# Two-layer decode step on one core: output weights fetched ahead, ScalarE and VectorE steps in another order, and TensorE's half key unit inside the prompt step

## The chip, the core and the metric

The kernel runs on one core of one Trainium2 chip. The metric is the device time of one execution in microseconds (us). Before the change it is 2687.8 us, the median of 3 runs (2681.95 to 2691.65).

## The reference, cut to what matters

Two layers; each computes a token branch (pooling in layer 0, stick-breaking attention in layer 1), a cross-attention over 256 memory tokens, gates both and projects the result back to the model width. The prompt has 1024 tokens; the sample group has 8 sequences of 4 tokens, each with 2048 past tokens whose keys and values lie in a paged cache.

```python
def sb_block(q_blk, qpos_blk, k, v, kpos, bias):
    z = einsum('bqhd,bkhd->bhqk', q_blk, k) * (HEAD_DIM ** -0.5) + bias
    mask = kpos[None, :] < qpos_blk[:, None]
    log_beta = log_sigmoid(z)
    log_rem = where(mask, log_beta - z, 0.0)
    later = cumsum(log_rem, axis=3, reverse=True) - log_rem
    a = where(mask, exp(log_beta + later), 0.0)
    return einsum('bhqk,bkhd->bqhd', a, v)

def merge_out(branch, gate, mq, mgate, mk, mv, g_q, w_out):
    q = rms_norm(mq, g_q)
    p = softmax(einsum('bqhd,bmhd->bhqm', q, mk) * (HEAD_DIM ** -0.5))
    mo = einsum('bhqm,bmhd->bqhd', p, mv)
    y = concatenate([branch * silu(gate), mo * silu(mgate)], axis=-1)
    return y @ w_out          # (tokens, 2048) @ (2048, 1024)
# x = x + merge_out(...), in both layers, for prompt and samples
```

There are 12 heads of width 128 in layer 1. Everything is float32; products that need it are made as three products of a rounded high part and a low rest (`hi*hi`, `lo*hi`, `hi*lo`).

## The kernel before, in words

The program runs phase after phase. Layer 0: input projection and pooling, `memory_attention_phase`, `out_phase`. Layer 1: `norm_phase`, `in_phase` (the projection, keys and values), `memory_attention_phase`, `stick_phase`, `out_phase`. Each phase is a block in which the five engines run their own program and wait on semaphores; the next block begins when all have ended. SyncE (SP) issues nearly all DMAs, in program order, so that a wait in its queue holds back everything behind it.

**out_phase** (L1182) is y @ w_out + x for 9 tiles of 128 tokens. TensorE multiplies 16 slices (`kk`) of the contraction, for each two halves of 512 columns with three products: 96 matmuls a tile. First `load_y(0)` fetches tile 0 of y and x; then w_out comes in 8 pieces of 1 MB through two buffers (`w`); ScalarE writes the high part of each piece (`w_hi`, L1241) and VectorE the rest (`w_lo`, L1254); the same is done for y once a tile (L1237, L1249). The weights are kept for all tiles. TensorE waits for `ylo` and, in tile 0, for each piece's `wlo`. A tile is loaded into the one buffer `y` when the rest of the tile before has been taken. Nothing of this begins before the phase.

**memory_attention_phase** (L794) fetches memory keys and values of the samples and, behind them, calls `following.fetch(sp)`: in layer 0 `NothingAhead`, in layer 1 `StickAhead` (L1476), which fetches what stick_phase needs first: the page table, query and key rows of head 0, the first key units (`keys`), then `vh`, `gh` and the new tokens' `kn`, `qn`, `vn`, the other key units and value pages. Its tile loop on ScalarE has exponentials (L975) of tile t+2, the copy of sample values `vev` (L991), and in every second tile the copy of the turned probabilities `pT` (L931); VectorE takes the other `pT` copies (L1051), the row maxima (L1017), the division (L1032) and the gate (L1038).

**stick_phase** (L1548) lays prompt and sample work side by side by one list `order`, written out before the program. The prompt has 144 steps P0 to P143, 12 for each head, of 128, 256, 384, 512, 128, 256, 384 columns and then five times 512. A step is: scores z of step t+2 (L2012), the triangle products which sum log terms (L2039, L2041 for the block before, L2046, L2049 for this one), and values of step t-1 (L2028). ScalarE does `evacuate(t+2)` (L1761, L1763: two reads of the score bank), `log_part(t+1)` (L1769, L1771), `high(t+1)` (L1789, rounded part of `spl`) and the exponential of step t (L1782). VectorE does `softplus(t+1)` (L1852), `exponent(t)` (L1870) and `low(t+1)` (L1861). For the samples there are 64 key units K in two halves (24 matmul pairs each, L2065, keys times queries into the one bank `krow`), the copy of that bank by ScalarE (`rows_out`, L1795, semaphore `rev`), its turning T (L2085), and 128 value pages V (6 matmuls each, L2107). One key unit goes with two prompt steps, so K lasts over P0 to P127; V begins at P14. SP fetches keys when VectorE has turned a unit (`ktr`) and a value page when TensorE has used one (`vdone`). The first half of K(u+1) overwrites `krow` and so waits for `rev` of unit u:

```python
                        if u:
                            pe.wait_ge(s["rev"], u)
```

The new tokens' scores (`new_tokens`, L2125) stand behind the first key half unit.

## Time and profile before

| | us |
|---|---|
| median of 3 runs | 2687.8 (2681.95 to 2691.65) |
| the profiled execution | 2685.2 |
| its span, first instruction to last | 2683.4 |
| memory attention of layer 0, TensorE's tiles | 609 to 673 |
| out_phase, layer 0: SP's first DMA, TensorE's first matmul, tile 1, end | 682.1, 696.2, 730.1, 905 |
| memory attention of layer 1, to its end | 1742 |
| stick_phase, TensorE | 1750.1 to 2447.5 |
| out_phase, layer 1: SP's first DMA, TensorE's first matmul, end | 2456.1, 2470.1, 2683 |
| TensorE busy | 2418.1 (90%) |
| VectorE, ScalarE busy | 988.4 (37%), 861.4 (32%) |

Times in the rows further down are counted from the start of the span. In a timeline row the first number is the start, the second how long the instruction (or the group under x) took, and in brackets stands the engine's idle time before it with what ended it. A matmul's duration includes its way through the array, so starts tell the pace better than durations. TensorE has 864 matmuls in each out_phase.

### The profile page before, as it was taken

How to read it: one execution, taken by the hardware profiler on the slowest of the kernel's cores; microseconds unless marked ns; L12 is line 12 of the kernel's file. 1: busy time of each engine (PE TensorE's matmuls, PEld its weight loads, DVE VectorE, ACT ScalarE, POOL GpSimd, SP SyncE). 2: the span in 40 equal slices, each digit the busy share in tenths (PEclk: the TensorE clock that was granted, in tenths of full speed). 3: DMA queues.
4: the chain of work that ended last, by engine and by line, in shares of the span. 5: the costliest groups of instructions: out<-in, count | busy, mean ns of one | idle time of the engine just before them, and what ended most of it. 6: DMA issues, size and time to landing. Idle time of an engine off the chain costs nothing. (4 is left out here: it accounts for less than half of the span.)

```text
span 2683.4 us, 42572 instructions
## 1 busy us (share of the span) xinstructions
PE 2418.1 (90%) x17253; PEld 2002.8 (75%) x17253; DVE 988.4 (37%) x1469; ACT 861.4 (32%) x1662; POOL 185.6 (7%) x377
## 2 busy tenths in 40 slices
PE   4699999998599699999999999779999999995999
PEld 4699999896488589999999998655555555542787
DVE  5421334105311321111112111467777777753211
ACT  4321111114210222112110011356666666674100
POOL 0000000102000000000001120211211111110000
PEclk8899999999799789999999998879999999998999
DMA  5422201302633232233231122658999999973432
GB/s 173 136 81 82 82 18 34 112 2 102 231 99 95 100 113 81 98 128 130 94 121 58 45 88 79 191 173 319 362 370 385 369 384 365 364 252 132 141 96 71
DMA packets 203708, 426.34 MB, mean 159 GB/s; under 512 B 22965, under 2 KB 116257, under 8 KB 203497
## 3 DMA queue, kind: packets, MB, share of 16 engines
q1 hardware_dynamic: 193209, 387.58, 41.3%
q0 software_dynamic: 10304, 36.05, 3.6%
q8 instruction: 136, 2.23, 0.3%
q14 instruction: 59, 0.48, 0.1%
HBM read 361.75 MB, written 62.37 MB: 158 GB/s over the span
## 5 line engine op out<-in xcount | busy, mean ns | idle before, releaser
L80 PE MATMUL o_bank<-o_w_hi,o_y_hi 128*128 128x512 f32 x576 | 228.9, 397 | 60.4 <-DVE o_w_lo L1254 59.5
L81 PE MATMUL o_bank<-o_w_lo,o_y_hi 128*128 128x512 f32 x576 | 227.4, 395 | 0.0
L82 PE MATMUL o_bank<-o_w_hi,o_y_lo 128*128 128x512 f32 x576 | 227.0, 394 | 0.0
L80 PEld LDWEIGHTS o_bank<-o_w_hi,o_y_hi 128*128 128x128 f32 x576 | 110.0, 191 | 88.8 <-issue 46.7
L1902 DVE STREAM_TRANSPOSE b_kt<-bf_kraw 128x768 f32<-128x768 f32 x172 | 166.2, 967 | 0.0
L1378 ACT ACTIVATE i_stage<-i_bank 128x352 f32<-128x352 f32 x108 | 50.1, 465 | 347.9 <-PE i_bank L82 347.9
L2065 PEld LDWEIGHTS b_krow<-b_kt,b_qd 128*32 128x32 f32 x3072 | 105.3, 111 | 70.0 <-issue 54.8
L80 PE MATMUL i_bank<-h_hT_hi,h_w_hi 128*128 128x352 f32 x432 | 140.7, 326 | 2.1 <-PEq L75 2.1
L2012 PE MATMUL b_zbank<-bf_qh,bf_kh 128*128 128x512 f32 (+3 forms) x288 | 134.2, 549 | 8.5 <-PEq L75 8.5
L80 PE MATMUL i_bank<-h_hT_hi,i_w_hi 128*128 128x352 f32 x432 | 141.1, 327 | 0.0
L2065 PE MATMUL b_krow<-b_kt,b_qd 128*32 128x128 f32 x3072 | 140.9, 280 | 0.0
L82 PE MATMUL i_bank<-h_hT_hi,i_w_lo 128*128 128x352 f32 x432 | 140.1, 324 | 0.0
L82 PE MATMUL i_bank<-h_hT_hi,h_w_lo 128*128 128x352 f32 x432 | 139.5, 323 | 0.0
L81 PE MATMUL i_bank<-h_hT_lo,h_w_hi 128*128 128x352 f32 x432 | 139.3, 323 | 0.0
L81 PE MATMUL i_bank<-h_hT_lo,i_w_hi 128*128 128x352 f32 x432 | 139.3, 322 | 0.0
L2107 PE MATMUL b_vout<-bf_vpage,b_daw 128*32 128x512 f32 x768 | 132.6, 597 | 0.0
L1237 ACT ACTIVATE o_y_hi<-o_y 128x2048 fp32r<-128x2048 f32 x18 | 34.5, 1916 | 297.4 <-DMA o_y<-scratch_yT 297.4
L1852 DVE SCALAR_TENSOR_TENSOR b_spl<-b_z,b_soft 128x512 f32<-128x512 f32 (+2 forms) x144 | 80.4, 558 | 127.9 <-ACT b_soft L1771 66.9
L82 PEld LDWEIGHTS o_bank<-o_w_hi,o_y_lo 128*128 128x128 f32 x576 | 110.1, 191 | 23.2
L2012 PEld LDWEIGHTS b_zbank<-bf_qh,bf_kh 128*128 128x128 f32 x288 | 44.3, 193 | 111.0 <-issue 108.7
L81 PEld LDWEIGHTS o_bank<-o_w_lo,o_y_hi 128*128 128x128 f32 x576 | 110.0, 191 | 22.8
L2028 PE MATMUL b_obank<-b_a,bf_vh 128*128 128x512 f32 (+3 forms) x288 | 119.3, 496 | 0.6 <-ACT b_a L1782 0.6
(308 smaller groups left out, 5567.0 us busy)
## 6 DMA issues: line engine op xcount, KB each, us to landing
bf_vpage<-in_cache_sb_v_dram SPq DMA_DIRECT2D x128, 768.0 KB, 7.2
bf_kraw<-in_cache_sb_k_dram SPq DMA_DIRECT2D x172, 384.0 KB
l_w<-in_cache_sb_k_dram SPq DMA_DIRECT2D x84, 384.0 KB
o_y<-scratch_yT SPq DMA_DIRECT2D x18, 1024.0 KB, 6.6
o_w<-in_w_out_dram SPq DMA_DIRECT2D x16, 1024.0 KB
l_w<-in_w_in_sb_dram SPq DMA_DIRECT2D x8, 1536.0 KB
i_w<-in_w_in_sb_dram SPq DMA_DIRECT2D x8, 1536.0 KB
l_w<-in_cache_mem_k_dram SPq DMA_DIRECT2D x16, 512.0 KB, 4.3
```

The source lines that it names most:

```text
L80: pe.matmul(out, stat_hi, mov_hi, start=first, stop=False)
L81: pe.matmul(out, stat_hi, mov_lo, start=False, stop=False)
L82: return pe.matmul(out, stat_lo, mov_hi, start=False, stop=last)
L1237: act.activation(y_hi[t % 2][:, :, :], y[:, :, :], ACT.Copy).then_inc(s["yhi"], 1)
L1378: act.activation(stage[:, b % 2, unit(n)], bank[(b % 2) * 3 + n][:, 0:TT], ACT.Silu if kind == "gate" else ACT.Copy).then_inc(s["evac"], 1)
L1852: dve.scalar_tensor_tensor(out=spl[:, 0:n], in0=z[:, t % 3, 0:n], scalar=0.0, in1=soft[:, t % 2, 0:n], op0=ALU.max, op1=ALU.add).then_inc( ...
L1902: dve.transpose(kt[u % 2][:, :, :, x * Q:(x + 1) * Q].rearrange("p h f j -> p (h f) j"), kraw[u % NK][:, x, :].rearrange("p (f j) -> p f j ...
L2012: ins = pe.matmul(zbank[t % 2][:, 0:n], kh[:, h % 2, kb * P:(kb + 1) * P], qh[:, h % 2, q0:q0 + n], start=True, stop=not diag, skip_group_ ...
L2028: pe.matmul(obank[:, 512 - n:512], vh[:, h % 2, kb, :], a[:, t % 3, 0:n], start=first, stop=last, skip_group_check=True).then_inc(s["pvd"], 1)
L2065: ins = pe.matmul(krow[pair * CT:(pair + 1) * CT, 0:P], qd[:, i % 2, at:at + CT], kt[u % 2][:, h, f, :], start=odd == 0 and f == 0, stop=o ...
L2107: ins = pe.matmul(vout[m * CT:(m + 1) * CT, :], daw[:, at, m * CT:(m + 1) * CT], vpage[n % NV][:, m * VC:(m + 1) * VC], start=n % PAGES == ...
```

## The change

- `out_phase` takes w_out in 16 pieces of 512 KB through five buffers (`RAW`): three lie in the layer's input weight buffer, which is free by then, two in a shared `Arena`. In `OutAhead.fetch` five pieces and 12 of the 16 slices of y's tile 0 (eight DMAs, 3.25 MB) are fetched ahead, and two pieces (`SPLIT`) and those slices are split ahead (`high` on ScalarE, `low` on VectorE). In layer 0 this stands in the memory attention: the fetch behind the memory DMAs, the splitting at the end of tiles t = 2 to 6. In layer 1 the fetch stands in stick_phase's SP list behind P130, ScalarE's part at P133 to P137, VectorE's at P134 to P138. The last four slices (in layer 1 slices 10 and 11, of the last head's two halves) come in out_phase.
- In `out_phase` the load of y's and x's tile 1 stands between pieces 10 and 11, its splitting before piece 13, and x's tile 0 last.
- `StickAhead.fetch` no longer fetches `vh`, `gh`, `kn`, `qn`, `vn`; `fetch_rest` does it as SP's first work in stick_phase.
- The buffers `kraw` and `kt` of stick_phase lie in the `Arena`.
- ScalarE's step is now log_part(t+1), exponential of t, high(t+1), evacuate(t+2); VectorE's takes exponent(t) before softplus(t+1).
- TensorE takes scores(t+2) alone, then the half key unit, then the rest of the step.

```diff
@@ class OutAhead
+        self.order = list(range(KM)) if i == 0 else list(range(10)) + [12, 13, 14, 15, 10, 11]
+        self.early, self.late = [([(0, 4), (4, 8), (8, 12)], (12, 16)), ([(0, 5), (5, 10), (12, 16)], (10, 12))][i]
+    def fetch(self, sp):
+        for at in range(SPLIT):
+            self.weights(sp, at)
+        for r in self.early:
+            self.rows(sp, r, self.yl)
+        for at in range(SPLIT, RAW):
+            self.weights(sp, at)
+    def high(self, act, t):
+        n = t - 2
+        if 0 <= n < SPLIT:
+            act.wait_ge(self.wl[n], 16)
+            act.activation(self.w_hi[n][:, :], self.w[n], ACT.Copy).then_inc(self.whi, 1)
+        if SPLIT <= n < SPLIT + len(self.early):
+            act.wait_ge(self.yl, 16 * len(self.early))
+            a, b = self.early[n - SPLIT]
+            act.activation(self.y_hi[:, a:b, :], self.y[:, a:b, :], ACT.Copy).then_inc(self.yhi, 1)
+    def low(self, dve, t):
+        n = t - 2
+        if 0 <= n < SPLIT:
+            dve.wait_ge(self.whi, n + 1)
...
@@ out_phase, SP
-                load_y(0)
-                for j in range(NW):
-                    if j >= 2:
-                        sp.wait_ge(s["wlo"], j - 1)
-                    sp.dma_start(w[j % 2][:, :, :], A["w_out"][i, j * CH * P:(j + 1) * CH * P, :].rearrange(
-                        "(k p) n -> p k n", p=P)).then_inc(wl[j % 2], 16)
-                load_y(1)
+                begun.rows(sp, begun.late, s["yl"])
+                for at in range(RAW, KM):
+                    sp.wait_ge(begun.wlo, at - RAW + 1)
+                    begun.weights(sp, at)
+                    if at == 2 * RAW:
+                        load_y(1)
+                load_x(0)
@@ out_phase, ScalarE (VectorE alike)
-                part(0)
-                for j in range(NW):
+                for at in range(SPLIT, KM):
+                    if at == RAW:
+                        part(0)
+                    if at == KM - 3:
+                        part(1)
@@ memory_attention_phase, end of a tile
+                    following.high(act, t)
+                    following.low(dve, t)
@@ stick_phase, SP
+                begun.fetch_rest(sp)
                 sp.dma_start(gs[:, :, :], S["gT"][:, :, SEQ:T].rearrange("h p t -> p h t")).then_inc(s["gsl"], 16)
+                    if e == ("P", NSTEP - 14):
+                        sp.wait_ge(s["ktr"], PG * NU)
+                        for n in range(2):
+                            sp.wait_ge(ys[n], 16 * 5)
+                        out.fetch(sp)
@@ stick_phase, ScalarE
                 def step(t):
-                    if t + 2 < NSTEP:
-                        evacuate(t + 2)
                     if t + 1 < NSTEP:
                         log_part(t + 1)
-                    if t + 1 < NSTEP:
-                        high(t + 1)
                     n = steps[t][4]
                     act.wait_ge(s["tsub"], t + 1)
                     act.activation(a[:, t % 3, 0:n], a[:, t % 3, 0:n], ACT.Exp).then_inc(s["ax"], 1)
+                    if t + 1 < NSTEP:
+                        high(t + 1)
+                    if t + 2 < NSTEP:
+                        evacuate(t + 2)
@@ stick_phase, VectorE
+                    exponent(t)
                     if t + 1 < NSTEP:
                         softplus(t + 1)
-                    exponent(t)
@@ stick_phase, TensorE
-                for e in order:
+                for n, e in enumerate(order):
                     if e[0] == "P":
-                        step(e[1])
+                        if e[1] + 2 < NSTEP:
+                            scores(e[1] + 2)
+                        if order[n + 1:n + 2] == [] or order[n + 1][0] != "K":
+                            step(e[1])
                     if e[0] == "K":
                         unit(e[1], e[2])
+                        if order[n - 1][0] == "P":
+                            step(order[n - 1][1])
```

TensorE in stick_phase, one step of 512 columns with a half key unit and a value page; before (`b_zbank` is the score bank, `b_cbank` the triangles' sum, `b_obank` the values, `b_krow` the key unit, `b_vout` the value page):

```order
L2012 MATMUL b_zbank<-bf_qh,bf_kh 128x512
L2039 MATMUL b_cbank<-b_spl_hi,b_before_r 128x512
L2041 MATMUL b_cbank<-b_spl_lo,b_before_r 128x512
L2046 MATMUL b_cbank<-b_spl_hi,b_suffix_r 128x512
L2049 MATMUL b_cbank<-b_spl_lo,b_suffix_r 128x512
L2028 MATMUL b_obank<-b_a,bf_vh 128x512
L2065 MATMUL b_krow<-b_kt,b_qd 32x128 x12
L2107 MATMUL b_vout<-bf_vpage,b_daw 32x512 x3
```

The same stretch now (the keys read from the arena):

```order
L2125 MATMUL b_zbank<-bf_qh,bf_kh 128x512
L2176 MATMUL b_krow<-ar_arena,b_qd 32x128 x12
L2150 MATMUL b_cbank<-b_spl_hi,b_before_r 128x512
L2152 MATMUL b_cbank<-b_spl_lo,b_before_r 128x512
L2157 MATMUL b_cbank<-b_spl_hi,b_suffix_r 128x512
L2160 MATMUL b_cbank<-b_spl_lo,b_suffix_r 128x512
L2141 MATMUL b_obank<-b_a,b_vh 128x512
L2218 MATMUL b_vout<-bf_vpage,b_daw 32x512 x3
```

The half key unit went from behind the values to between the scores and the triangles.

ScalarE in stick_phase, from a step's logarithm to the copy of a key unit (`b_soft`, `b_z` the two reads of the scores, `b_spl_hi` the rounded part, `b_a` the exponential, `b_kev` the key unit's copy); before:

```order
L1771 ACTIVATE b_soft<-b_soft 128x512
L1789 ACTIVATE b_spl_hi<-b_spl 128x512
L1782 ACTIVATE b_a<-b_a 128x512
L1795 ACTIVATE b_kev<-b_krow 96x128
L1799 ACTIVATE b_dx<-b_dx 128x384
```

Now:

```order
L1878 ACTIVATE b_soft<-b_soft 128x512
L1885 ACTIVATE b_a<-b_a 128x512
L1896 ACTIVATE b_spl_hi<-b_spl 128x512
L1868 ACTIVATE b_soft<-b_zbank,c_rowb 128x512
L1870 ACTIVATE b_z<-b_zbank,c_rowb 128x512
L1902 ACTIVATE b_kev<-b_krow 96x128
L1906 ACTIVATE b_dx<-b_dx 128x384
```

The rounded part and the two reads of the next scores now stand between the exponential and the copy of the key unit.

ScalarE in layer 0's memory attention, now (`a_e` the exponentials of a tile's four heads, `a_pT` a copy of turned probabilities, `a_vev` a copy of sample values, `ar_w_hi` and `ar_y_hi` high parts of a weight piece and of slices of y):

```order
L975 ACTIVATE a_e,a_sums<-a_bank,a_nb,a_st 128x256 x4
L1243 ACTIVATE ar_w_hi_4487<-l_w 128x1024
L931 ACTIVATE a_pT<-a_bank 128x512
L975 ACTIVATE a_e,a_sums<-a_bank,a_nb,a_st 128x256 x4
L991 ACTIVATE a_vev<-a_bank 128x512
L1243 ACTIVATE ar_w_hi_4488<-l_w 128x1024
L931 ACTIVATE a_pT<-a_bank 128x512
L975 ACTIVATE a_e,a_sums<-a_bank,a_nb,a_st 128x256 x4
L1247 ACTIVATE ar_y_hi<-ar_arena 128x512
```

Before, the same rows stand there without L1243 and L1247.

## Rows read from the trace of the kernel before

**Rows 1.** The page: busy time by engine; the 40 slices of the span.

```profile
PE 2418.1 (90%) x17253; PEld 2002.8 (75%) x17253; DVE 988.4 (37%) x1469; ACT 861.4 (32%) x1662; POOL 185.6 (7%) x377
...
GB/s 173 136 81 82 82 18 34 112 2 102 231 99 95 100 113 81 98 128 130 94 121 58 45 88 79 191 173 319 362 370 385 369 384 365 364 252 132 141 96 71
```

**Rows 2.** Busy time by stretch; behind POOL: granted PE clock, DMA share, GB/s.

```profile
2048.00:2335.00 287.00, 274.54 (x3277) 155.90 (x3265) 212.21 (x339) 191.31 (x417) 42.50 (x109) 1.00 0.98 375
...
2102.86:2160.30 57.44, 54.86 (x667) 31.48 (x664) 43.17 (x70) 38.23 (x84) 5.60 (x13) 1.00 0.97 362
```

**Rows 3.** What SP's queue waited for, 1850 to 2350: us in total, times, longest.

```profile
SPq L1511 <- PE b_vout L2107: 139.4, 56, 4.2
```

**Rows 4.** Timeline, out_phase of layer 0: SP, ScalarE, TensorE.

```profile
682.11 0.38 SPq L1209 DMA_DIRECT2D o_y<-scratch_yT  x1
...
694.39 1.91 ACT L1241 ACTIVATE o_w_hi<-o_w 128x2048 fp32r<-128x2048 f32 x1 [0.62 <-DMA o_w<-in_w_out_dram]
...
696.24 0.76 PE L80 MATMUL o_bank<-o_w_hi,o_y_hi 128*128 128x512 f32 x1 [23.22 <-DVE o_w_lo L1254]
...
727.62 0.39 PE L81 MATMUL o_bank<-o_w_lo,o_y_hi 128*128 128x512 f32 x1
...
729.21 0.39 PE L82 MATMUL o_bank<-o_w_hi,o_y_lo 128*128 128x512 f32 x1
730.06 0.50 PE L80 MATMUL o_bank<-o_w_hi,o_y_hi 128*128 128x512 f32 x1 [0.46 <-DVE o_y_lo L1249]
```

**Rows 5.** Timeline, out_phase of layer 1: SP, TensorE, VectorE.

```profile
2456.05 0.38 SPq L1209 DMA_DIRECT2D o_y<-scratch_yT  x1
...
2470.10 0.77 PE L80 MATMUL o_bank<-o_w_hi,o_y_hi 128*128 128x512 f32 x1 [22.62 <-DVE o_w_lo L1254]
...
2502.99 2.29 DVE L1249 TENSOR_TENSOR o_y_lo<-o_y,o_y_hi 128x2048 fp32r<-128x2048 f32 x1 [1.28 <-ACT o_y_hi L1237]
```

**Rows 6.** Timeline of VectorE, memory attention of layer 0.

```profile
652.17 0.69 DVE L1051 COPY a_pT<-a_bank 128x512 f32<-128x512 f32 x1 [0.18 <-PE a_bank L1165]
```

**Rows 7.** Timeline, memory attention of layer 1: TensorE, SP.

```profile
1720.50 3.64 PE L1131 MATMUL a_bank<-a_sq,a_psT 128*32 128x512 f32 x16 [8.05 <-DMA a_sq<-in_cache_mem_v_dram]
...
1686.43 0.44 SPq L1526 DMA_DIRECT2D bf_vh<-out_sbv_p_dram  x1
...
1695.01 4.09 SPq L1506 DMA_DIRECT2D bf_kraw<-in_cache_sb_k_dram  x4
...
1706.84 3.19 SPq L948 DMA_DIRECT2D a_sq<-in_cache_mem_v_dram  x4
```

**Rows 8.** Timeline of TensorE, stick_phase.

```profile
1758.52 1.49 PE L2125 MATMUL b_sbank<-bf_vpage 128*32 128x32 f32 x24
...
2150.61 1.13 PE L2012 MATMUL b_zbank<-bf_qh,bf_kh 128*128 128x512 f32 x2
...
2152.50 1.02 PE L2028 MATMUL b_obank<-b_a,bf_vh 128*128 128x512 f32 x2
2153.45 0.97 PE L2065 MATMUL b_krow<-b_kt,b_qd 128*32 128x128 f32 x21
...
2158.44 1.07 PE L2065 MATMUL b_krow<-b_kt,b_qd 128*32 128x128 f32 x24
2159.34 1.03 PE L2107 MATMUL b_vout<-bf_vpage,b_daw 128*32 128x512 f32 x6
2160.30 0.49 PE L2012 MATMUL b_zbank<-bf_qh,bf_kh 128*128 128x128 f32 x2
```

**Rows 9.** Timeline, stick_phase: ScalarE (first row the key copy), then VectorE.

```profile
2161.15 0.25 ACT L1795 ACTIVATE b_kev<-b_krow 96x128 f32<-96x128 f32 x1
...
2434.91 0.63 ACT L1789 ACTIVATE b_spl_hi<-b_spl 128x512 fp32r<-128x512 f32 x1 [0.81 <-DVE b_spl L1852]
...
2439.29 0.63 ACT L1789 ACTIVATE b_spl_hi<-b_spl 128x512 fp32r<-128x512 f32 x1 [0.81 <-DVE b_spl L1852]
...
2439.17 0.68 DVE L1870 TENSOR_TENSOR b_a<-b_z,b_cbank 128x512 f32<-128x512 f32 x1
```

More of the change, by code:

```diff
@@ L1194, in out_phase @@
         x = k.sb("x", [P, 2, D])
         bank = k.ps("bank", 4)
-        wl = [k.sem(f"wl{n}") for n in range(2)]
         xl = [k.sem(f"xl{n}") for n in range(2)]
         ol = [k.sem(f"ol{n}") for n in range(2)]
-        s = {n: k.sem(n) for n in "yl whi wlo yhi ylo ready added".split()}
+        s = {n: k.sem(n) for n in "yl yhi ylo ready added".split()}
         N = TILES + 1
-        NW = KM // CH
         tok = lambda t: t * P if t < TILES else LAST
+        part_of = lambda t: slice(0, KM) if t else slice(*begun.late)
@@ L1614, in stick_phase @@
         a = k.sb("a", [P, 3, 512])
-        kt = [k.sb(f"kt{n}", [P, HH, HD // Q, P]) for n in range(2)]
         qd = k.sb("qd", [P, 2, HEADS * QP])
```

168 lines of the change are left out of this document (117 added, 51 removed).

## The prediction

> **What bounds the kernel now.** I read the page first: TensorE is busy 90% of the span [rows 1], so time can be won only where it stands still or where its own work shrinks, and the change removes no matmul. Then the stretches: in the long middle of stick_phase TensorE is busy 274.5 of 287 us, ScalarE two thirds, VectorE three quarters, and the DMA engines show a share of 0.98 at 375 GB/s [rows 2]. So there both TensorE and the transfers are near full. The queue's waits say which leads: SP waits 139 us of 500 for TensorE to have used a value page before it may fetch the next [rows 3]; the transfers wait for the compute, not the reverse. Then the timelines at the seams: TensorE stands 23.2 us ahead of out_phase in layer 0 [rows 4] and 22.6 us in layer 1 [rows 5], both for the first rest of a weight piece, and 8.05 us in layer 1's memory attention for a DMA [rows 7]. These are the large holes. A difference of 0.3%, 8 us, is about what a measurement of this kernel can tell from none.
>
> **The change part by part**, in us against the profiled execution (2685.2; the median is 2.6 above it).
>
> *Memory attention, layer 0: +6.* New there: two weight pieces and 12 slices of y, each split in ScalarE and VectorE. ScalarE takes 1.91 for 1 MB [rows 4], so about 0.95 for a piece and 0.48 to 0.5 for four slices of y; VectorE's rest takes 2.29 for 1 MB [rows 5], so 1.15 and 0.6. VectorE's rest of tile t waits for ScalarE's high part, which stands behind that engine's exponentials of tile t+2; behind VectorE's rest stands its copy of the turned probabilities, which today starts 0.18 after it has nothing else to do [rows 6], and TensorE waits for that copy. Walking the five tiles gives 1.3, 3.3, 0, 2.3 and 0.4 behind t = 2 to 6; sum 7.3, less about 1 which the tiles that ScalarE copies give back: 6. Bounds: 0 if the slack in the tiles takes all, and 9, all five high parts and rests in a row (2 times 2.1 and 3 times 1.1 is 7.5) and the DMA issues behind them.
>
> *out_phase, layer 0: -18.* SP begins at 682.11, TensorE at 696.24, and tile 1 starts at 730.06 [rows 4]. Now two pieces and y are ready, and TensorE begins at about 682.3. The pace is 7 matmuls in 1.59, 0.227 each [rows 4], 21.8 for 96. But it needs data: still to come are 11 pieces of 0.52 MB, 0.26 MB of y, and 1.57 MB for tile 1, 7.6 MB. The 3.67 MB before were issued at 682.11 and the last was there at 694.39 [rows 4]: 299 GB/s with the start-up in it, and 385 GB/s is the highest slice of the page [rows 1]. That is 20 to 25 us, and the split of the last piece (0.95 and 1.15) and its six matmuls (1.4) come after it: 705.6 to 711 for the end of tile 0. Five buffers pass slowly where piece 11 waits behind tile 1's y and x (1.57 MB, 4.5 us) and where tile 1's split (1.91 and 2.29) stands before piece 13; walked through buffer by buffer it gives 5.6 of stalls above 21.8 and a slow start of 1.8 to 2: 711.7. So 730.06 becomes about 712, -18. Bounds -24 (no stall) and -8 (start at the full 14 us earlier, half of it lost to the supply).
>
> *Memory attention, layer 1: -6.* SP issued vh, gh, kn, qn, vn from 1686.43 to 1695.01, about 8 with their waits, and only at 1706.84 the next memory values [rows 7], for which TensorE waited until 1720.50, idle 8.05 [rows 7]. They go out 8 earlier, so the idle shrinks to about 2; the rows behind are unchanged. Bounds -8 and 0.
>
> *Start of stick_phase: +2.* The moved loads are now the block's first DMAs, and new_tokens at 1758.52 [rows 8] needs three of them. Issued from 1750 on, five DMAs in some 8 us as before, they land near 1760.5. Bounds 0 and +6.
>
> *P0 to P13: 0*, between -3 and +3: no value pages, TensorE waits for the first steps' chain anyway, and this chain has the same members.
>
> *P14 to P127, keys and values: +13.* This is the term that decides least clearly. The new order of ScalarE puts the rounded part of step t+1 and two reads of step t+2 between the exponential and the key copy; the new order of TensorE puts the next key half unit ahead of the triangles. The first half of K(u+1) waits for the copy of K(u). So a loop arises over a pair of steps. From K(u+1)'s first half: 0.90 (2158.44 to 2159.34) [rows 8], triangles 0.93, values 0.95 (2152.50 to 2153.45), turned rows 0.3, a value page 0.96 (2159.34 to 2160.30), scores and triangles of the next step 1.89 (2150.61 to 2152.50) and the second half unit 0.90: 6.84. From there to the copy: semaphore 0.20, exponent to exponential 0.72 (from 2439.17 to the end of the rounded part that starts at 2439.29, 0.6), the exponential 0.6, rounded part 0.6 and two reads of 0.6 less what they overlap, 1.14 (between 2434.91 and 2439.29 there are six such instructions and 0.81 idle, 0.6 each) [rows 9], the copy 0.25 [rows 9] and semaphores 0.17: 3.6. The loop is 10.4 for two full steps; TensorE took 9.69 for them from 2150.61 to 2160.30 [rows 8]. With the narrower steps of a head the same walk gives 8.9, 8.6, 8.9, 9.7, 10.4 and 9.4, 55.9, and with the sample sums (2.25) and the select (0.7), which stand in the loop too, 58.8 against 57.44 [rows 2]: +1.4 a head, 9.5 heads, +13. Bounds: below, the idle of a head (57.44 less 54.86 [rows 2], 2.6) vanishes, which is what the new order of the exponent and of ScalarE gives if the copy never comes late, -25; above +25, if every head loses a further 1.3 to bubbles. I take the walk, since it rests on durations of these same instructions.
>
> *P128 to P143: -3.5.* Without keys ScalarE sets the pace: 4.38 a full step, of which 0.81 is a wait for spl [rows 9]. With the exponential of t before the rounded part the wait is covered: 3.77, 0.6 a step, -8 over ten full and six narrower. Against it ScalarE gets two pieces (0.95 each) and three parts of y (0.65, 0.65, 0.55): 3.75, and VectorE a little: +4.5. The 3.25 MB fetched at P130 take about 9 us of transfers ahead of the last pages; SP has some five steps of pages in buffers (19 to 22 us), so it stays hidden. If it did not, +4.
>
> *out_phase, layer 1: -19.5.* As in layer 0, from 2456.05; tile 0 took until 2505.3 (the rest of y at 2502.99 and its 2.29) [rows 5]. 2456.2 and 29.5 is 2485.7. Bounds -25 and -9.
>
> *Blocks and semaphore clears: +1.* A few more clears of some 0.1 each.
>
> Sum: 6 - 18 - 6 + 2 + 0 + 13 - 3.5 - 19.5 + 1 = -25. Against the median: 2662.8, rounded to **2662**.
>
> **A rule against the trace.** In the middle of stick_phase the trace shows 375 GB/s over 287 us and slices up to 385 [rows 1, 2]. The Trainium skill, "DMA: Bandwidth & Descriptors", section "Where 436 GB/s comes from", says that for transfers between HBM and SBUF the HBM side binds, at about 358 GB/s for a core. The trace does not agree: it lies 5% over it. By that rule the stretch could gain nothing from any order of instructions, which is the second rival below, reached by another way.
>
> **The rivals.**
> - *The copy never comes late.* The six steps' buffers and the half unit's 0.9 cover the copy, and TensorE runs without gaps. For: the walk has 0.7 of lateness in the full pairs and little in the narrow ones. Against: TensorE's busy 95% leaves 2.6 a head, and at this pace pages would have to come at 375 times 57.4/54.9, 392 GB/s, above every slice of the page. Price -25 for +13: total -63, **2625**.
> - *The stretch does not move.* Transfers at a share of 0.98 [rows 2] set the pace whatever TensorE does, or lateness and gain cancel. For: share and rate; against: SP's 139 us of waits for TensorE [rows 3]. Price 0 for +13: **2650**.
> - *Supply limits both out starts.* The pieces of 512 KB come no faster than those of 1 MB, and tile 0 is as long as before, only begun 14 earlier. Then each start gains 14 less some loss, 13: about 11.5 less gain in the two: **2674**.
> - *Slower: the half key unit lengthens each step's own loop.* Triangles of step t+1 now always have 0.90 of key work before them, and the loop triangle, exponent, exponential, rounded part, rest runs through every step. Where the loop already bounds, 0.4 of the 0.9 (the rest covers what TensorE waited for) comes on each of 114 steps, +46 for +13: total +8, **2695**. It decides once the rounded part's chain, 3.5 to 3.6, together with the key half and triangles exceeds the step of 4.8 that TensorE needs itself [rows 8]; 3.6 and 1.8 is 5.4, but only if the chain begins behind the triangles and not, as I read the order, from the step before. Against it: log and reads of a step are two steps ahead.
> - That the change does not do what it says (the early pieces not ready at the out start) would leave the starts as they are: part of the third.
>
> **How the numbers follow.** My forecast 0.52; no move of the stretch 0.20; TensorE without gaps 0.10; supply 0.10; the slower case 0.08. The forecast alone spans 2648 to 2676 (its terms' bounds taken two at a time). The range should hold 8 in 10: it takes in the stretch unmoved and the supply case and leaves out the two ends: 2638 to 2682. Faster by over 0.3% is below 2679.7: the forecast, the second, the first and most of the supply case: 0.86. Within 0.3%: 0.08, from the upper tails of the forecast and of supply. Slower: 0.06, most of the last case.
>
> **What would show it.** TensorE's first matmul of either out_phase within 1 us of SP's first DMA there, and tile 1 some 29 us later. In the middle of stick_phase a new idle of TensorE ahead of the first key half, released by ScalarE's copy, about 0.7 in full pairs, and heads of 58.8 with SP waiting more for TensorE than now; heads of 54.9 would prove the first rival, heads of 57.4 the second, and idle ahead of the triangles (for the rest of spl) in every step the slower case. In the tail full steps of 3.8. In memory attention of layer 0 five idles of TensorE behind VectorE's or ScalarE's split, together 6; in layer 1 an idle of 2 for 8. I am wrong if the middle moves by more than 25 either way, or if an out start gains less than 8.

## The result: slower by 0.7%, with the half key unit as the cause

| | before | after |
|---|---|---|
| median of 5 runs, us | 2687.8 (2681.3 to 2691.7) | 2705.0 (2696.9 to 2711.2) |
| ratio | | 1.0068, 95% interval 1.0042 to 1.0095 |
| profiled execution, us | 2685.2 | 2711.2 |
| its span, us | 2683.4 | 2709.5 |

The prediction was 2662 in a range of 2638 to 2682, with 0.06 for slower: it was wrong in sign and size. The profiled execution after lies 6 us above its median, the one before 2.6 below; the comparison of the two traces (26.1 us of span) therefore overstates the change by some 9 us.

Two rows of the page after, the answer to [rows 1]. TensorE is busy 38 us longer with the same 17253 matmuls, and the slices of the middle moved 331 to 365 GB/s where they had moved 362 to 385.

```profile
PE 2455.7 (91%) x17253; PEld 2006.6 (74%) x17253; DVE 988.4 (36%) x1491; ACT 857.7 (32%) x1684; POOL 188.9 (7%) x377
...
GB/s 171 136 79 81 81 26 25 111 22 130 184 93 101 103 111 95 111 104 127 95 115 58 66 55 153 216 173 301 343 337 365 331 364 334 349 247 193 144 100 65
```

The waits of TensorE after, from 1850 to 2350 (us in total, times, longest):

```profile
PE b_krow L2176 <- ACT b_kev L1902: 35.6, 29, 2.3
```

The same view of the kernel before: there it waited for something else.

```profile
PE b_cbank L2049 <- DVE b_spl_lo L1861: 20.7, 39, 0.7
PE b_cbank L2039 <- DVE b_a L1870: 1.8, 8, 0.2
```

So the old wait (the triangles for the rest of spl) is gone, and a larger one stands in its place: the key unit for ScalarE's copy of the one before. The waits of SP after, over the same stretch, answer to [rows 3]: the queue waited longer for TensorE, 170 us for 139. The transfers became slower because the compute did.

```profile
SPq L1611 <- PE b_vout L2218: 170.4, 70, 4.7
```

The seams after, SP and TensorE of both output phases, answer to [rows 4, 5], and the first scores of stick_phase:

```profile
690.67 0.38 SPq L1228 DMA_DIRECT2D ar_arena<-scratch_yT  x1
...
690.87 0.76 PE L80 MATMUL o_bank<-ar_w_hi,ar_y_hi 128*128 128x512 f32 x1 [8.46 <-PEq L75]
...
711.58 0.50 PE L80 MATMUL o_bank<-o_w_hi,ar_y_hi 128*128 128x512 f32 x1 [2.41 <-DVE o_w_lo L1340]
716.86 0.62 PE L80 MATMUL o_bank<-o_w_hi,ar_y_hi 128*128 128x512 f32 x1 [2.22 <-DVE o_w_lo L1340]
...
722.30 1.31 DVE L1349 TENSOR_TENSOR o_x<-o_bank,o_x 128x512 f32<-128x512 f32 x2 [3.22 <-PE o_bank L82]
...
1737.73 0.77 PE L2125 MATMUL b_zbank<-bf_qh,bf_kh 128*128 128x128 f32 x2 [8.46 <-PEq L75]
...
2497.86 0.76 PE L80 MATMUL o_bank<-ar_w_hi,ar_y_hi 128*128 128x512 f32 x1 [8.80 <-PEq L75]
...
2527.36 1.31 DVE L1349 TENSOR_TENSOR o_x<-o_bank,o_x 128x512 f32<-128x512 f32 x2 [1.68 <-PE o_bank L82]
```

TensorE begins 0.2 us behind SP's first DMA instead of 14, and tile 0 ends 31.6 and 29.7 us behind that DMA, where it took 47.8 and 49.2. The stalls of 2.41 and 2.22 for the rest of a weight piece are those that the prediction walked through (4.6 together, where it had 5.6). All this worked. The loss is in between: stick_phase's TensorE went from 697 us (1750.1 to 2447.5) to 751 (1737.7 to 2489.1).

A full step of 512 columns with half a key unit and a value page, before (TensorE); it ends at 2160.30 [rows 8], after 4.71 us:

```profile
2155.59 1.12 PE L2012 MATMUL b_zbank<-bf_qh,bf_kh 128*128 128x512 f32 x2
```

The same step takes 5.05 after the change, with no idle time in it:

```profile
2179.54 1.13 PE L2125 MATMUL b_zbank<-bf_qh,bf_kh 128*128 128x512 f32 x2
2180.60 1.07 PE L2176 MATMUL b_krow<-ar_arena,b_qd 128*32 128x128 f32 x24
2181.60 0.50 PE L2150 MATMUL b_cbank<-b_spl_hi,b_before_r 128*128 128x512 f32 x1
2181.94 0.40 PE L2152 MATMUL b_cbank<-b_spl_lo,b_before_r 128*128 128x512 f32 x1
...
2183.60 1.06 PE L2218 MATMUL b_vout<-bf_vpage,b_daw 128*32 128x512 f32 x6
2184.59 0.49 PE L2125 MATMUL b_zbank<-bf_qh,bf_kh 128*128 128x128 f32 x2
```

The key group took 0.90 from its start to the next group's and now takes 1.00; scores and triangles took 1.90 together and now take 2.11, the page 0.96 and now 0.99. These 0.34 us a full step are the first of three losses. The second is the wait; ScalarE after, around the copy of a key unit, with the end of the triangles (the values behind them start) and the VectorE work ahead of its first row, and the key group that waits for the copy (TensorE):

```profile
2139.61 0.38 PE L2141 MATMUL b_obank<-b_a,b_vh 128*128 128x128 f32 x2
2140.03 0.97 DVE L2012 STREAM_TRANSPOSE ar_arena<-ar_arena 128x768 f32<-128x768 f32 x1
2140.92 0.38 DVE L1980 TENSOR_TENSOR b_a<-b_z,b_cbank 128x256 f32<-128x256 f32 x1
2141.34 0.42 ACT L1885 ACTIVATE b_a<-b_a 128x256 f32<-128x256 f32 x1 [1.12 <-DVE b_a L1980]
2141.80 0.52 ACT L1896 ACTIVATE b_spl_hi<-b_spl 128x384 fp32r<-128x384 f32 x1
2142.23 0.67 ACT L1868 ACTIVATE b_soft<-b_zbank,c_rowb 128x512 f32<-128x512 f32 x1
2142.80 0.68 ACT L1870 ACTIVATE b_z<-b_zbank,c_rowb 128x512 f32<-128x512 f32 x1
2143.37 0.27 ACT L1902 ACTIVATE b_kev<-b_krow 96x128 f32<-96x128 f32 x1
...
2143.78 1.90 PE L2176 MATMUL b_krow<-ar_arena,b_qd 128*32 128x128 f32 x24 [2.31 <-ACT b_kev L1902]
2145.60 0.58 PE L2150 MATMUL b_cbank<-b_spl_hi,b_before_r 128*128 128x256 f32 x1
```

And the third: that key group took 1.82 us instead of 1.00. Busy time by stretch after says why; the column behind POOL is the granted clock:

```profile
2136.00:2141.00 5.00, 5.00 (x62) 2.38 (x48) 4.97 (x10) 2.60 (x6) 0.00 (x0) 1.00 0.98 351
...
2143.80:2145.60 1.80, 1.80 (x24) 1.42 (x24) 0.97 (x2) 1.74 (x4) 0.22 (x1) 0.52 0.91 324
2145.60:2147.90 2.30, 2.30 (x43) 1.89 (x43) 1.30 (x3) 0.41 (x2) 1.81 (x7) 0.64 0.97 341
```

After an idle of 2.31 the granted clock was 0.52 for 1.80 us, close to the lower of TensorE's two levels (1.2 GHz), and 0.64 on the mean of the next 2.30, before it was back at 2.4 GHz. From 1790 to 2430 seven key groups stand behind an idle of 2.3 to 3.5, and six of them show it; the six behind 1.7 to 1.9 do not. In heads 1 to 10 (a head is one of the twelve rounds of 12 prompt steps) the clock stood at its lower level for 27.3 us, before the change for 3.4. The idle's length alone does not decide: before the change the one fall in these heads came behind an idle of 1.74.

### The profile page after: what moved, and what is told of

Its sections match the earlier page's. It is cut to its first block and busy times, and to the rows that moved or that the text cites. A ratio compares the mean times of both kernels' runs of the same rounds, so it can differ in the third digit from the quotient of the medians.

```text
span 2709.5 us, 42694 instructions
## 1 busy us (share of the span) xinstructions
PE 2455.7 (91%) x17253; PEld 2006.6 (74%) x17253; DVE 988.4 (36%) x1491; ACT 857.7 (32%) x1684; POOL 188.9 (7%) x377
## 5 line engine op out<-in xcount | busy, mean ns | idle before, releaser
L2176 PE MATMUL b_krow<-ar_arena,b_qd 128*32 128x128 f32 x3072 | 145.8, 286 | 63.9 <-ACT b_kev L1902 62.6
L2176 PEld LDWEIGHTS b_krow<-ar_arena,b_qd 128*32 128x32 f32 x3072 | 110.4, 114 | 119.8 <-issue 113.2
L2012 DVE STREAM_TRANSPOSE ar_arena<-ar_arena 128x768 f32<-128x768 f32 x172 | 166.1, 967 | 0.0
L2141 PE MATMUL b_obank<-b_a,b_vh 128*128 128x512 f32 (+3 forms) x288 | 119.9, 498 | 0.6 <-ACT b_a L1885 0.6
L80 PE MATMUL o_bank<-o_w_hi,ar_y_hi 128*128 128x512 f32 x280 | 112.7, 402 | 8.0 <-DVE o_w_lo L1340 8.0
L81 PE MATMUL o_bank<-o_w_lo,ar_y_hi 128*128 128x512 f32 x280 | 112.3, 401 | 0.0
L82 PE MATMUL o_bank<-o_w_hi,ar_y_lo 128*128 128x512 f32 x280 | 112.2, 401 | 0.0
L80 PE MATMUL p_bank<-h_hT_hi,h_w_hi 128*128 128x352 f32 x288 | 94.3, 328 | 0.0
L80 PE MATMUL p_bank<-h_hT_hi,p_w_hi 128*128 128x352 f32 x288 | 93.7, 325 | 0.0
L82 PE MATMUL p_bank<-h_hT_hi,h_w_lo 128*128 128x352 f32 x288 | 93.6, 325 | 0.0
```

The lines of the kernel that those rows point to most:

```text
L80: pe.matmul(out, stat_hi, mov_hi, start=first, stop=False)
L81: pe.matmul(out, stat_hi, mov_lo, start=False, stop=False)
L82: return pe.matmul(out, stat_lo, mov_hi, start=False, stop=last)
L2012: dve.transpose(kt[u % 2][:, :, :, x * Q:(x + 1) * Q].rearrange("p h f j -> p (h f) j"), kraw[u % NK][:, x, :].rearrange("p (f j) -> p f j ...
L2141: pe.matmul(obank[:, 512 - n:512], vh[:, h % 2, kb, :], a[:, t % 3, 0:n], start=first, stop=last, skip_group_check=True).then_inc(s["pvd"], 1)
L2176: ins = pe.matmul(krow[pair * CT:(pair + 1) * CT, 0:P], qd[:, i % 2, at:at + CT], kt[u % 2][:, h, f, :], start=odd == 0 and f == 0, stop=o ...
```

## The experiments

Three theories stood at first. **A**: two causes, TensorE's own work grows by its new order, and the copy is late. **B**: the copy alone. **C**: neither, but what was moved in transfers and memory. All runs are judged against the kernel before, run beside them (2682 to 2684 us). "Head" is the time of one head in stick_phase, from its first scores to the next head's; head 6 of the kernel before is 57.4, after 62.7 (empty where stick_phase is not at issue).

| kernel | median, us | ratio, 95% interval | head 6 | TensorE's largest wait, 1850 to 2350 |
|---|---|---|---|---|
| e1_old_pe | 2619.8 | 0.9763 (0.9747 to 0.9780) | 55.6 | rest of spl, 4.6 |
| e2_old_act_dve | 2677.4 | 0.9978 (0.9968 to 0.9987) | 59.1 | turned keys, 19.5 |
| e3_stream_only | 2658.4 | 0.9906 (0.9889 to 0.9922) | 57.4 | rest of spl, 20.5 |
| e4_copy_early | 2650.5 | 0.9876 (0.9859 to 0.9892) | 58.1 | turned keys, 9.6 |
| e5_key_behind_tri | 2661.1 | 0.9924 (0.9899 to 0.9948) | 59.4 | rest of spl, 7.2 |
| e6_key_first | 2669.2 | 0.9948 (0.9934 to 0.9962) | 57.9 | turned keys, 30.9 |
| e7_act_order_only | 2668.4 | 0.9955 (0.9929 to 0.9980) | 56.7 | rounded part, 8.3 |
| e8_dve_order_only | 2636.8 | 0.9831 (0.9800 to 0.9863) | 55.9 | rest of spl, 8.0 |
| e9_low_later | 2615.6 | 0.9742 (0.9719 to 0.9765) | | |
| e10_all_between | 2680.2 | 0.9988 (0.9977 to 0.9999) | 59.8 | turned keys, 51.0 |
| e11_orders_only | 2650.6 | 0.9873 (0.9850 to 0.9896) | 55.6 | rest of spl, 4.6 |
| e12_pad32 | 2612.7 | 0.9731 (0.9717 to 0.9745) | | |

### e1_old_pe: TensorE's order back, the rest stays

```diff
                         if e[1] + 2 < NSTEP:
                             scores(e[1] + 2)
-                        if order[n + 1:n + 2] == [] or order[n + 1][0] != "K":
-                            step(e[1])
+                        step(e[1])
                     if e[0] == "K":
                         unit(e[1], e[2])
-                        if order[n - 1][0] == "P":
-                            step(order[n - 1][1])
```

> The change with TensorE's half key unit back behind the whole step; ScalarE's and VectorE's new order and the streamed weights stay. Theory A (two causes: TensorE's own work grows by some 0.3 us a step because the half key unit has new neighbours, 55.6 to 58.5 busy in a head of 62.7, and the wait for the key copy adds some 2 us a head): both go, since the copy now has the whole step's rest before the next unit; heads of 57.4 or less, total 2705 - 10 x 5.3 = about 2650. Theory B (only ScalarE's new order makes the copy late): the wait stays in part, heads of 60 and more, total 2675 or more. Theory C (the slower part is not in the order but in the transfers, by what was moved or by the arena): heads stay at 62, total 2700.

It runs in 2619.8, 85 us under the change and 62 under the kernel before. B and C are out in this form: heads fell to 55.6, below both kernels, and SP's fetches were no obstacle. A has the direction, but its 2650 is 30 too high: it took the new orders of ScalarE and VectorE as worth nothing, and so heads of 57.4. TensorE's waits in the middle are nearly nothing:

```profile
PE b_cbank L2160 <- DVE b_spl_lo L1971: 4.6, 15, 0.3
PE b_cbank L2157 <- ACT b_spl_hi L1896: 4.3, 10, 0.6
```

### e2_old_act_dve and e3_stream_only: the other parts apart

Both put back the order of ScalarE and VectorE; e3 also that of TensorE.

```diff
                 def step(t):
+                    if t + 2 < NSTEP:
+                        evacuate(t + 2)
                     if t + 1 < NSTEP:
                         log_part(t + 1)
+                    if t + 1 < NSTEP:
+                        high(t + 1)
...
-                    if t + 1 < NSTEP:
-                        high(t + 1)
-                    if t + 2 < NSTEP:
-                        evacuate(t + 2)
@@ VectorE
-                    exponent(t)
                     if t + 1 < NSTEP:
                         softplus(t + 1)
+                    exponent(t)
```

> The change with ScalarE's and VectorE's order of before; TensorE's new order and the streamed weights stay. Theory A: the copy stands right behind the exponential again, so the wait of TensorE's key unit for it falls from 62.6 us to under 15, but TensorE's own 0.3 us a step stays: heads of about 60, total about 2680 to 2690. Theory B: all goes, heads of 57.4, total about 2655. Theory C: no change, about 2705.

> The streamed weights alone: all three engines of stick_phase in the order of before, with the moved loads and the arena. Theories A and B: stick_phase as before plus its late first loads, the seams keep what they gained (12.3 us up to stick_phase, 15.5 in the last output phase): about 2660. Theory C: heads stay at 62, about 2710.

The streamed weights alone give 2658.4, 23 to 24 us less than before, with heads as before: A's number, and the arena costs stick_phase nothing. TensorE's new order costs 19 us with the old orders of the other two engines and 85 with the new ones. So the parts don't add: each of the two reorderings makes the other worse, since one asks for the key copy earlier and the other makes it later. In e2 the wait for the copy is gone, as A said (its 2680 to 2690 is 3 above the 2677.4), but one for turned keys took its place (groups of instructions of e2, TensorE, 1850 to 2350; behind the second bar the idle before them):

```profile
L2176 PE MATMUL b_krow<-ar_arena,b_qd 128*32 128x128 f32 x2400 | 107.4, 275 | 19.8 <-DVE ar_arena L2012 19.5
```

### e4_copy_early: the wait for the copy taken away, TensorE's order kept

```diff
+                    if t % 2 and t // 2 < NU:
+                        rows_out(t // 2)
                     n = steps[t][4]
                     act.wait_ge(s["tsub"], t + 1)
                     act.activation(a[:, t % 3, 0:n], a[:, t % 3, 0:n], ACT.Exp).then_inc(s["ax"], 1)
...
-                    if e[0] == "K" and e[2] == 1:
-                        rows_out(e[1])
```

> The change with ScalarE's copy of a key unit moved up, from behind the reads of the next scores to ahead of the exponential. TensorE's order is untouched. Theory A: the wait for the copy goes (62.6 us to under 5), TensorE's own work stays at 58.5 a head: heads of about 60, total about 2680. Theory B: heads of 57.4 or less, about 2650. Theory C: about 2705.

2650.5: 54.5 less than the change, and 30.7 more than e1. That parts the two causes as A has it. The first number is the copy's wait with the slower clock behind it; the second is what TensorE's order costs by itself, with no wait for the copy: ten heads took 582.4 here, 556.2 in e1 and 631.1 after the change. A had forecast 2680; it had put the worth of the wait too low. B's number, 2650, came true, but not its mechanism: it had heads of 57.4 or less because TensorE's order costs nothing, and they take 58.1, where e1's take 55.6. Of the 26.2 between e4 and e1 only 2.8 are idle time (14.4 in e4's ten heads, mostly for turned keys, and 11.6 in e1's); the rest is TensorE's own time.

### e5_key_behind_tri and e6_key_first: which neighbours cost

Both build on e4. In e5 the half key unit stands behind the triangles, and only the step's values come behind it. In e6 it stands first, and the scores come behind it as well. This is e6's edit; e5's moves `values` out of the step in the same way and isn't shown.

```diff
-                        if e[1] + 2 < NSTEP:
-                            scores(e[1] + 2)
                         if order[n + 1:n + 2] == [] or order[n + 1][0] != "K":
+                            if e[1] + 2 < NSTEP:
+                                scores(e[1] + 2)
                             step(e[1])
@@ behind unit(...)
                         if order[n - 1][0] == "P":
+                            scores(order[n - 1][1] + 2)
                             step(order[n - 1][1])
```

> As e4_copy_early (copy of the key unit ahead of the exponential, so no wait for it), with the half key unit one place further back: between triangles and values. It tells what the 0.3 us a step of TensorE's own work are. Theory J1 (the scores hide the triangles' first weight load only where they stand right ahead of them; the keys in between uncover it): the price goes, full steps of 4.7, heads of 55.6 to 56.5, total about 2625. Theory J2 (any 128x128 weights behind the short key matmuls are uncovered, the values' as well as the triangles'): the price stays, full steps of 5.0, heads of 58, total about 2650. Theory J3 (scores followed by keys, two float32 products in a row, are what costs): it goes as well, as J1; e6_key_first parts it from J1.

> As e4_copy_early, with the half key unit one place further forward: ahead of the scores, so that the step begins with it and scores stand next to the triangles. Theory J1: no price, full steps of 4.7, total about 2625, if the earlier key unit waits for nothing new. Theory J2: the scores' weights stand behind the short key matmuls, full steps of 4.9 to 5.0, total about 2645. Theory J3: scores followed by keys are gone, no price, 2625.

e5 keeps the price, e6 does not: J1 and J3 fell with e5 (both had it at 2625, it is at 2661), J2 with e6, whose steps without a wait are as long as e1's. The two kinds that can be compared have the turning of key rows in them: 4.15 to 4.18 and 4.96 in e6, 4.18 and 4.99 in e1, 4.45 and 5.31 in e5. e6's loss is another: the earlier key group waits for VectorE's turned keys, 30.9 us in 500. From these rows came a fourth rule: count how often the 32-column products (keys `b_krow`, pages `b_vout`) and the 128-column ones (scores, triangles, values) follow each other. In e6 (TensorE) the page takes 0.86 to the start of the keys, and the keys 1.01 to the start of the scores:

```profile
2064.89 1.06 PE L2218 MATMUL b_vout<-bf_vpage,b_daw 128*32 128x512 f32 x6
2065.75 1.08 PE L2176 MATMUL b_krow<-ar_arena,b_qd 128*32 128x128 f32 x24
2066.76 1.12 PE L2125 MATMUL b_zbank<-bf_qh,bf_kh 128*128 128x512 f32 x2
2067.32 0.62 PE L2130 MATMUL b_zbank<-b_neg_r,b_ident_r 128*128 128x128 f32 x1
```

### e10_all_between: the rule put to the test

As e4, with the page beside the key unit between scores and triangles.

```diff
                     if e[0] == "P":
                         if e[1] + 2 < NSTEP:
                             scores(e[1] + 2)
-                        if order[n + 1:n + 2] == [] or order[n + 1][0] != "K":
-                            step(e[1])
+                        rest = e[1]
+                    elif e[0] in "NCS" and rest is not None:
+                        step(rest)
+                        rest = None
...
+                    if rest is not None and (order[n + 1:n + 2] == [] or order[n + 1][0] == "P"):
+                        step(rest)
+                        rest = None
```

> As e4_copy_early, with the value page as well as the half key unit between scores and triangles, in all steps without sample sums or select. It tests what the four places of the key unit so far leave: behind the values (e1: full step 4.71) and ahead of the scores (e6: 4.98 where e1 has 4.98) no price, between scores and triangles or between triangles and values 0.32 a step. Theory J4: every change between products with 32-column weights (keys, pages) and those with 128-column weights (scores, triangles, values) costs about 0.16, and there are two in a step where keys and page stand together, four where they stand apart. Here there are two: full steps of 4.7, TensorE's busy time per head back to that of e1, total 2625 unless the triangles, now behind the page, make a new wait. Theory J5: a half key unit behind the scores or ahead of anything with 128-column weights costs by itself: full steps of 4.9 to 5.0, total 2650.

The total, 2680.2, is not J4's 2625, because the wait for turned keys grew to 51.0 us in 500. TensorE's own pieces are as J4 has them. The table gives the median time from a group's start to the next group's, where there is no wait, with what follows in brackets. e6's row is put together from groups of different steps, since each of its full steps with these five groups alone ends in a wait for turned keys:

| | scores | triangles | values | half key unit | page | sum | changes |
|---|---|---|---|---|---|---|---|
| e1 | 0.56 (triangles) | 1.33 | 0.95 (keys) | 0.90 (page) | 0.96 | 4.70 | 2 |
| e6 | 0.56 (triangles) | 1.33 | 0.95 (page) | 1.00 (scores) | 0.86 (keys) | 4.70 | 2 |
| e10 | 0.95 (keys) | 1.03 | 0.86 (scores) | 0.90 (page) | 0.96 (triangles) | 4.70 | 2 |
| e4 | 1.06 (keys) | 1.04 | 0.95 (page) | 1.00 (triangles) | 0.99 | 5.04 | 4 |
| e5 | 0.56 (triangles) | 1.42 (keys) | 1.06 (page) | 1.00 (values) | 0.99 | 5.03 | 4 |

Two changes give 4.70 in three quite different orders, four give 5.03 and 5.04: two more changes between 32 and 128 columns of weights cost 0.33, 0.16 each on the mean. In e10 that is four of the nine full steps (4.71); the other five, 4.81, stand behind a page, which makes one change more. Over heads 1 to 10 TensorE's time without waits is 551.4 in e10, 544.7 in e1 and 568.1 in e4; e10's holds 34.1 us at the lower clock level, of which e1 has none. J5 is out. This is shown for these groups. Keys and pages share more than the width of their weights (both are the samples' work), and no run parts the one from the other; why a change costs it is not shown either. The Trainium skill, "TensorE: Matmul & The Clock Gate", section "LDWEIGHTS (loading the stationary operand)", says that the time of a weight load goes by its columns. The trace agrees in direction (on the page of before, 191 ns for a load of 128 columns and 111 for one of 32), and a wide load behind products with 32 columns of weights may have less to hide under; that is a guess, which no run here tests.

### e7_act_order_only and e8_dve_order_only: which order gained

Each is e3 with one of the two new orders, ScalarE's in e7, VectorE's in e8.

> Streamed weights and ScalarE's new order; TensorE's and VectorE's orders as before. The two orders together gained 38.6 us (2658.4 to 2619.8), by TensorE's wait for the rest of spl (20.7 us of 500 before, 4.6 after). Theory V (VectorE's order does it: the exponent no longer stands behind softplus): ScalarE's order alone gains under 10, 2650 or more. Theory S (ScalarE's order does it: rounded part and reads no longer ahead of the exponential): 2625 to 2630. Theory B2 (both are needed, since the exponential early needs the exponent early): under 10 alone for each.

> Streamed weights and VectorE's new order; TensorE's and ScalarE's orders as before. Theory V: 2620 to 2630. Theory S: 2650 or more. Theory B2: 2650 or more, or slower than 2658, since softplus now stands behind an exponent that waits for the triangles while ScalarE's rounded part, ahead of the exponential, waits for softplus.

From e3's 2658.4: VectorE's order alone 21.6 less, ScalarE's alone 10 more, both 38.6 less. V had VectorE's order at 2620 to 2630 (2636.8 measured) and ScalarE's under 10 of gain; it is the nearest theory, but each needs the other for the whole. S and B2 (VectorE's order alone under 10) are out. TensorE's waits in e7 from 1850 to 2350 show what ScalarE's order alone does: its rounded part now stands behind an exponential that still comes late.

```profile
PE b_cbank L2157 <- ACT b_spl_hi L1896: 8.3, 20, 0.5
PE b_cbank L2160 <- DVE b_spl_lo L1971: 5.6, 26, 0.2
PE b_cbank L2150 <- DVE b_a L1980: 2.7, 7, 0.5
```

These waits are 16.6 together and e3's 22.6, so they don't account for the 10 us that e7 is slower. Heads 1 to 10 are 6.3 longer in e7 with less idle time in them (21.7 for 28.5); what makes the matmuls take longer there is open (idles under 0.15 us are not counted as such).

### e11_orders_only: without streamed weights

The kernel before with both new orders of ScalarE and VectorE, and nothing else.

> The kernel before with the new orders of ScalarE and VectorE alone: no streamed weights, no arena, TensorE as before. If the two parts add: 2682 less 38.6 = 2643. If the orders only pay behind the moved loads or the earlier fetch: 2670 or more.

2650.6, 33 less than the kernel before, where 38.6 were to come if the parts added; most of it adds. Its middle moved (busy time by stretch, last two columns the DMA share and GB/s):

```profile
1850.00:2350.00 500.00, 491.06 (x5944) 283.81 (x5947) 383.34 (x615) 343.44 (x761) 81.95 (x199) 1.00 1.00 382
```

### e9_low_later: the memory attention of layer 0

```diff
-                    following.low(dve, t)
+                    following.low(dve, t - 1)
```

> e1_old_pe (2619.8) with the early rests of VectorE in layer 0's memory attention moved one tile later, so that VectorE no longer waits for ScalarE's high part ahead of its copy of the turned probabilities. Theory M (that wait is what makes this phase 8 to 9 us longer): the phase ends 4 to 7 us earlier, total about 2615. Theory N (the split work itself or the transfers fetched there cost it): it stays, about 2620.

2615.6; out_phase of layer 0 begins at 685.76 instead of 690.72 in e1, 5.0 earlier. Theory M holds for the phase; in the median the step is 4.2, inside the spread of the two. The waits of TensorE there (615 to 690), first in e1, where VectorE's copy of the turned probabilities `a_pT` comes late:

```profile
PE a_bank L1178 <- issue: 4.1, 3, 3.0
PE a_bank L1167 <- issue: 4.0, 1, 4.0
PE a_bank L1178 <- DVE a_pT L1052: 3.5, 1, 3.5
```

and in e9, where the wait for VectorE's copy is gone and one for ScalarE's stands there:

```profile
PE a_bank L1167 <- issue: 4.0, 1, 4.0
PE a_bank L1178 <- ACT a_pT L931: 3.8, 2, 2.6
...
PE a_bank L1178 <- issue: 0.8, 1, 0.8
```

### e12_pad32: an unused buffer of 32 bytes

```diff
+        Kit(nc, ctx, "pad_", "right").sb("pad", [P, 8])
         for i in range(2):
             with ExitStack() as lctx:
```

> e9_low_later (2615.6) with an unused buffer of 32 bytes in each partition at the top of SBUF, so that the arena, the layer's weight buffer and the input projections' rows begin at a multiple of 64 bytes (today 32 beyond one). After the change the matmuls of the output phases stand 0.233 us apart where they read rows or weights from the arena and 0.227 where they don't; before, all at 0.227. Theory P (the place of the operand within 64 bytes): all stand 0.227 apart, 3.3 us less in each output phase, and the projections, whose rows lie the same way, get shorter as well by up to 17; total 2592 to 2609. Theory Q (it is the region or something else, not the alignment): the pace stays at 0.233, total 2616.

2612.7 against e9's 2615.6, their intervals overlap: no difference that can be told. Theory P is out as put: the matmuls of tiles whose y lies in the arena still stand 0.233 apart (0.234 in e9), and the output phase's eight later tiles take 177.1 instead of 177.5. That is Q's case.

## Why the prediction was wrong

Measured in the two traces (predicted in brackets):

| part | after less before, us |
|---|---|
| up to the memory attention of layer 0 | +1.5 (0) |
| memory attention, layer 0 | +7.1 (+6) |
| out_phase, layer 0: tile 0 | -16.2 (-18) |
| out_phase, layer 0: the other tiles | +3.3 (0) |
| between | +1.0 (0) |
| memory attention, layer 1 | -8.9 (-6) |
| head 0 of stick_phase | +4.0 (+2) |
| heads 1 to 10 | +52.1 (+13) |
| the tail, head 11 | -2.1 (-3.5) |
| out_phase, layer 1: tile 0; the other tiles | -19.4; +3.9 (-19.5; 0) |
| sum, before rounding | +26.1 (-25 with clears) |

The prediction had said that it would be wrong if the middle moved by more than 25; it moved by 52.

**The step that failed is the term on P14 to P127.** Its mechanism was right: a loop of a pair of steps through the key copy, which stands behind the rounded part and two reads. Its size, +13, was 39 too low. The walk gave a head of 58.8; heads 1 to 10 took 63.1 on the mean. Split by TensorE's idle time they read:

| heads 1 to 10, us | in all | idle | without the idle |
|---|---|---|---|
| before | 579.0 | 28.2 | 550.9 |
| e1 (TensorE's old order) | 556.2 | 11.6 | 544.7 |
| e4 (new order, copy early) | 582.4 | 14.4 | 568.1 |
| after | 631.1 | 50.9 | 580.2 |

The walk carried TensorE's own times over unchanged, so it had 0 for the last column and its +13 was all idle; measured are +29.3 and +22.8. Three things were mis-sized.

1. *The pieces of TensorE were priced where they stood before.* 6.84 us of the loop were summed from starts of the old order, and the same durations were carried to the new one. The order itself made four changes of weight width out of two, 0.33 a full step; over ten heads it costs 23.4 of TensorE's own time (e4 less e1). Here is a full pair after the change: from the first half unit to the end of the triangles it takes 7.36 (to 2182.65), where 6.84 were summed, and from there through exponent, exponential, rounded part, reads and copy to the next key unit 3.61, where 3.6 were. The loop is 10.97 for 10.4, and all of the miss is TensorE's part:

```profile
2175.29 1.07 PE L2176 MATMUL b_krow<-ar_arena,b_qd 128*32 128x128 f32 x24
...
2182.65 1.02 PE L2141 MATMUL b_obank<-b_a,b_vh 128*128 128x512 f32 x2
...
2186.26 1.07 PE L2176 MATMUL b_krow<-ar_arena,b_qd 128*32 128x128 f32 x24 [1.12 <-ACT b_kev L1902]
```

2. *The narrow pairs were taken to have little lateness.* 32 of the 50.9 us of idle stand ahead of the third and the seventh step of a head, behind steps of 128 and 256 columns, in idles of 0.7 to 3.5. Where they are 1.7 or more, TensorE's part of the loop is short (6.2), and the chain behind it takes 4.2 instead of 3.6: in the rows from 2139.61 on, in the section on the result, the triangles end at 2139.61, but the exponent starts at 2140.92, since VectorE was still busy with the samples' work and with turning keys. The walk had not put that work into the chain.
3. *The clock was left out.* With 27.3 us at the lower level in these heads, for 3.4 before and in e4, half speed costs up to 12 us, by estimate (24 us more at half the clock); the time without idle is 12.1 longer after the change than in e4.

Against these three stands a gain that the prediction didn't price by itself: with the new orders of ScalarE and VectorE alone the wait for the rest of spl nearly goes, and TensorE's other time falls by 6.2 as well (e1 less before; why is open). So the change as a whole lost what these orders win (38.6 us in the whole) and more. The prediction's nearest rival, the slower one, came near the size by luck: its 0.4 a step is +46, but by another mechanism (a longer loop of each step), and that loop did not appear, since after the change TensorE has no wait for spl in the middle.

Copy wait and clock together are the 54.5 us between the change and e4. Two slips of the working are small beside this: the seven terms of the chain sum to 3.68 and not 3.6, and 2662.8 was rounded to 2662.

**What was right.** The two starts of the output phases (tile 0 to 2 us), their stalls, the memory phases to 3 us and the tail to 1.4. Left out were the later tiles of the output phases, +3.3 and +3.9; 3.0 of each is the pace of their matmuls (177.5 us for 174.4).

**The rivals.** The first (TensorE without gaps, 2625) got 0.10, and it is nearly what the two orders do when TensorE's is left alone: e1, 2619.8, with 1.2 us of idle a head. The argument against it, that the transfers would have to run at 392 GB/s, was wrong: e1's heads of 55.6 ran at 377, and e11 shows 382 over 500 us. The Trainium skill's limit of about 358 for a core ("DMA: Bandwidth & Descriptors", "Where 436 GB/s comes from") is passed by these runs further than by the kernel before. The second rival (the stretch unmoved) and the third (supply) did not occur. The slower rival was right in sign, and near in size by luck. What would have shown the term before the run: the value of the old wait (20.7 us of 500 for the rest of spl) set beside the order of each step, as a gain to be kept, and the start-to-start times of a group sorted by the group that follows it; the kernel before shows already that a group's time depends on its neighbour, with full triangles of 1.33 right behind the scores and 0.99 behind the mask's product.

## What to carry to other kernels

Price a moved group of matmuls with its new neighbours: here two more changes between narrow and wide weights cost 0.33 us a full step, so work of one weight width belongs together. Put every piece of each engine on the loop into the walk, the other work in its queue too, and most of all where the steps are short. When one engine's order is moved, compare the walk also with the pace that the rest of the change would reach without it, and not only with the old one. And try the parts of a combined change apart: here three of its four parts together give 2619.8 where all four give 2705.0, and with one splitting step put a tile later 2615.6, 2.6% under the kernel before.

## What the runs showed that was not expected

- Changes between products with 32-column and 128-column weights cost about 0.16 us each on the mean: full steps of 4.70 with two, 5.03 and 5.04 with four.
- DMA at 382 GB/s over 500 us with a share of 1.00 (e11).
- In the output phases every second tile, whose y lies in the arena, and the first pieces have matmuls some 0.233 apart, the others 0.227 as before. It makes 3.0 us in each of the two phases. Shifting the arena by 32 bytes did not cure it; the cause stays open, and no other layout was tried.
- After the change the granted clock fell behind six of seven idles of 2.3 to 3.5 us, and behind none of six of 1.7 to 1.9. The other runs show that the length alone doesn't tell: in e6 it fell behind four of ten idles of 2.0 and not behind one of 2.62, in e10 behind three of five of 2.14 and four of six of 2.7 to 3.0.
